# Gate table stored in stages of 64 tokens, kept activations stored from GpSimd's queue through three buffers

## The reference, cut to what matters

```python
def one(xb):
    qry = (xb @ wq).reshape(blk, PEER_HEADS, 2, PEER_DHALF)
    sc = jnp.einsum('thpd,hpkd->thpk', qry, subkeys).astype(F32)
    s1, i1 = lax.top_k(sc[:, :, 0], PEER_TOPK)
    s2, i2 = lax.top_k(sc[:, :, 1], PEER_TOPK)
    ...
    eid = e1 * PEER_NKEYS + e2
    g = jax.nn.softmax(sf, axis=-1)
    ug = jnp.take(u_tab, eid, axis=0)
    vg = jnp.take(v_tab, eid, axis=0)
    act = jax.nn.gelu(jnp.einsum('td,thkd->thk', xb, ug).astype(F32))
    return jnp.einsum('thk,thkd->td', (g * act).astype(xb.dtype), vg)
```

## Time and profile before

| what | value |
|---|---|
| median of 3 runs | 4225.2 us (4215.39 to 4245.17) |
| the profiled execution | 4207.73 us |
| its span, first to last instruction | 4206.1 us |
| mean granted TensorE clock | 0.962 of full speed |
| TensorE busy | 3867.2 us (92%) |
| VectorE busy | 2655.8 us (63%) |
| ScalarE busy | 1184.2 us (28%) |
| GpSimd busy | 671.5 us (16%) |
| the table of gates, gate_all | 28 stores of 2048 KB, 128 loads of 448 KB |
| the table of activations, act_all | 80 stores and 80 loads of 448 KB |

### The profile page before, as it was taken

How to read it: one execution, slowest core, us unless ns; L and a number is a source line. 1 busy time by engine, 2 the same in 40 slices (tenths; PEclk the granted TensorE clock), 3 DMA queues, 4 the chain that set the end, 5 groups by cost and what they waited for, 6 DMA issues and landing times. The chain is left out here.

```text
span 4206.1 us, 57139 instructions
## 1 busy us (share of the span) xinstructions
PE 3867.2 (92%) x21916; PEld 2051.7 (49%) x21916; DVE 2655.8 (63%) x4847; ACT 1184.2 (28%) x1707; POOL 671.5 (16%) x536
## 2 busy tenths in 40 slices
PE   5999787599969799989999997999999999999997
PEld 3676343166634544445555553444444444444443
DVE  5133111477655501989899975878777777777776
ACT  4233111144343301334334332222222222222223
POOL 0000000133201000000000002211111144444431
PEclk9999898799889899999999999999999999999999
DMA  5232541723163213889998879999999899999994
GB/s 206 95 118 79 148 120 46 267 78 100 55 217 130 88 52 103 218 236 293 290 269 239 228 215 280 276 253 246 240 246 245 230 271 289 274 288 284 274 254 122
DMA packets 975371, 837.17 MB, mean 199 GB/s; under 512 B 753730, under 2 KB 825754, under 8 KB 967707
## 3 DMA queue, kind: packets, MB, share of 16 engines
q1 hardware_dynamic: 912180, 564.40, 52.2%
q0 software_dynamic: 58960, 211.32, 14.8%
q10 hardware_dynamic: 4032, 58.72, 3.5%
HBM read 616.00 MB, written 181.85 MB: 190 GB/s over the span
## 5 line engine op out<-in xcount | busy, mean ns | idle before, releaser
L2920 PE MATMUL ex_psy<-ex_vhi,ex_wboth 128*128 128x512 f16 x3584 | 1077.3, 380 | 19.1 <-DVE ex_wboth L2779 13.5
L2888 PE MATMUL ex_psa<-h_hi,ex_uth 128*128 128x512 f16 (+1 forms) x2048 | 726.1, 355 | 33.7 <-DMA ex_utl<-ex_ulo 26.3
L2888 PE MATMUL ex_psa<-h_lo,ex_uth 128*128 128x512 f16 (+1 forms) x2048 | 725.7, 354 | 0.0
L2888 PE MATMUL ex_psa<-h_hi,ex_utl 128*128 128x512 f16 (+1 forms) x2048 | 725.2, 354 | 0.0
L2920 PE MATMUL ex_psy<-ex_vlo,ex_wboth 128*128 128x512 f16 x1792 | 681.1, 380 | 0.0
L2920 PEld LDWEIGHTS ex_psy<-ex_vhi,ex_wboth 128*128 128x128 f16 x3584 | 351.4, 98 | 444.3 <-DVE ex_wboth L2779 13.9
L2431 POOL DMA_INDIRECT ex_ug<-in_peer_u_dram,ex_idxp x128 | 152.4, 1190 | 1485.2 <-DVE ex_ug L2744 1063.4
L2740 DVE TENSOR_TENSOR ex_acc<-ex_acc,ex_psy 128x512 f32<-128x512 f32 x434 | 292.0, 682 | 145.3 <-PE ex_psy L2920 145.3
L2469 ACT ACTIVATE ex_wa<-ex_psa 128x512 f32<-128x512 f32 (+1 forms) x256 | 134.7, 542 | 671.9 <-PE ex_psa L2888 512.4
L2888 PEld LDWEIGHTS ex_psa<-h_hi,ex_uth 128*128 128x128 f16 x2048 | 201.0, 98 | 218.0 <-DMA ex_utl<-ex_ulo 29.4
L2888 PEld LDWEIGHTS ex_psa<-h_hi,ex_utl 128*128 128x128 f16 x2048 | 201.1, 98 | 190.0 <-issue 5.0
(11 more groups left out here) (387 smaller groups left out, 6108.1 us busy)
## 6 DMA issues: line engine op xcount, KB each, us to landing
ex_u<-in_peer_u_dram SPq DMA_DIRECT2D x128, 512.0 KB, 6.1
ex_v<-in_peer_v_dram SPq DMA_DIRECT2D x128, 512.0 KB, 5.6
gate_all<-rt_stage ACTq DMA_DIRECT2D x28, 2048.0 KB, 8.1
ex_gate<-gate_all SPq DMA_DIRECT2D x128, 448.0 KB, 7.7
act_all<-ex_wa SPq DMA_DIRECT2D x80, 448.0 KB, 3.3
ex_wa<-act_all SPq DMA_DIRECT2D x80, 448.0 KB, 5.5
ad_w<-in_ada_w_dram SPq DMA_DIRECT2D x8, 2048.0 KB, 10.3
sh_w<-in_w_in_dram SPq DMA_DIRECT2D x10, 1024.0 KB, 8.2
```

The source lines that it names most:

```text
L2888: mm = nc.tensor.matmul(ps_a[:, at:at + e - a], x[s][:, k, :], h[:, k, a:e], start=(k == 0 and j == 0), stop=(k == KD - 1 and j == 2))
L2920: mm = nc.tensor.matmul(sum_bank(q, n), w, v_[:, a * 512:(a + 1) * 512], start=(j == 0), stop=(j == len(mms) - 1))
```

## The change

1. `RUN` becomes 64: `gate_all` has 14 stages of 64 tokens, a stage buffer holds 8 groups, a store is 4096 KB (32 KB a partition), and there are 14 stores. A block's gates are read as 128 x 14 pieces of 256 bytes.
2. `keep` leaves SP. GpSimd's queue issues the 80 stores to `act_all`, in order, each behind its gelu. 
3. `wa` has a third buffer during the slots (`wa_third`); the gelu of block eb waits for the store of block eb - 3.
4. GpSimd comes to its first gathers only behind the 80 stores, and waits there also for the last evacuation (`evac`) and for both stage buffers to be stored. The six gathers of batch 0 move from slot 2 to group 0.
5. To make room, `cand` and `same` share their space (VectorE alone writes and reads both, in order), and `wa` and `st` move out of the region that the routing's buffers share.

```diff
--- before.py
+++ after.py
@@ -38,7 +38,7 @@
 NCH = P // CH
 HEADS, KEYS, TOPK, DHALF = 8, 128, 16, 128
 PICKS = HEADS * TOPK
-RUN = 32
+RUN = 64
 NEG = -1e30
 REC = DH + 2
 C_Q, C_K, C_V = 0, AW, 2 * AW
@@ -2209,8 +2209,9 @@
     YB = 4
     more = lambda eb, n: not isinstance(eb, int) or eb + n < KEYS
     two = lambda name: [pr.sem(f"ex_{name}{s}") for s in range(2)]
-    u_in, ut_in, g_in, wa_in, wa_stored = two("uin"), two("utin"), two("gin"), two("wain"), two("wastored")
+    u_in, ut_in, g_in, wa_in = two("uin"), two("utin"), two("gin"), two("wain")
     v_in = two("vin")
+    wa_stored = [pr.sem(f"ex_wastored{s}") for s in range(3)]
     (u_hi_done, u_lo_done, acted, gelu_done, w_done, w_hi_done, w_lo_done, v_hi_done, v_lo_done,
      y_done, added, ready) = (pr.sem(f"ex_{n}") for n in (
          "uhi", "ulo", "acted", "gelu", "w", "whi", "wlo", "vhi", "vlo", "y", "added", "ready"))
@@ -2241,18 +2242,22 @@
         gate_s, gate_up = sb("gates", [P, PAIRS]), sb("gateup", [NS, PAIRS])
         gate_g = sb("gateg", [P, PAIRS, 3])
         dots, gelus, weights = (sb(n, [P, 2 * EB, 3]) for n in ("dots", "gelus", "weights"))
+        wa = [sb(f"wa{s}", [P, DENSE]) for s in range(2)]
+        st = sb("st", [P, 6, PT + 1])
         with ExitStack() as early:
             ea = lambda name, shape, dt=F32: early.enter_context(nc.sbuf_tensor(f"rt_{name}", shape, dt))
             stage = [ea(f"stage{s}", [P, KEYS, RUN]) for s in range(2)]
+            wa_third = ea("wathird", [P, DENSE])
             sc, sc2 = ea("sc", [P, HP, KEYS]), ea("sc2", [P, HP, KEYS])
             top, ix = ea("top", [P, HP, TOPK]), ea("ix", [P, HP, TOPK], U32)
             ixf = ea("ixf", [P, HP, TOPK])
-            cand = ea("cand", [P, HEADS, TOPK * TOPK])
+            with nc.sbuf_tensor("rt_cand", [P, HEADS, TOPK * TOPK], F32) as cand:
+                pass
+            same = ea("same", [P, 2, HEADS, TOPK, TOPK], F16)
             best, ci = ea("best", [P, HEADS, TOPK]), ea("ci", [P, HEADS, TOPK], U32)
             c1, c2 = ea("c1", [P, HEADS, TOPK], U32), ea("c2", [P, HEADS, TOPK], U32)
             place = ea("place", [P, 2, HEADS, TOPK], F16)
             numbers = ea("numbers", [P, 2, HEADS, TOPK, TOPK], F16)
-            same = ea("same", [P, 2, HEADS, TOPK, TOPK], F16)
             ranks = ea("ranks", [P, TOPK, TOPK], F16)
             e12 = ea("e12", [P, 2, PICKS])
             ex, gate_t = ea("ex", [P, HEADS, TOPK]), ea("gatet", [P, HEADS, TOPK])
@@ -2268,9 +2273,8 @@
             v_hi, v_lo = ([sb(f"{n}{s}", [P, D], F16) for s in range(2 * EB)] for n in ("vhi", "vlo"))
             w_both = [sb(f"wboth{s}", [P, 2 * DENSE], F16) for s in range(2 * EB)]
             u, u_hi, u_lo, ut_h, ut_l = turns
-            wa = [sb(f"wa{s}", [P, DENSE]) for s in range(2)]
-            st = sb("st", [P, 6, PT + 1])
             ug, vg = ([sb(f"{n}{r}", [P, D]) for r in range(3)] for n in ("ug", "vg"))
+            wa_kept = wa + [wa_third]
             x_at = [u[0], u[1], ug[0], ug[1]]
             fg = ug[2]
             norm_rows = lambda p: P if NORM_M[p] < PT else NS
@@ -2338,10 +2342,6 @@
                         sp.wait_ge(sc_free, n)
                     r, a = rows_in(n), ROUTE[n] * P
                     sp.dma_start(sc[0:r, :, :].rearrange("p a k -> p (a k)"), t["scores"][a:a + r, :]).then_inc(sc_in, 16)
-
-                def keep(eb):
-                    sp.wait_ge(gelu_done, eb * 2 + 6)
-                    sp.dma_start(act_all[eb], wa[eb % 2][:, :]).then_inc(wa_stored[eb % 2], 16)
 
                 copies = window_copies(pr)
                 load_scores(0)
@@ -2357,13 +2357,9 @@
                         sp.wait_ge(picked, 7)
                         sp.dma_start(idx_s[NS:P, :], idx_up[:, :]).then_inc(moved, 16)
                         sp.dma_start(gate_s[NS:P, :], gate_up[:, :]).then_inc(moved, 16)
-                    if eb >= 2:
-                        keep(eb - 2)
                     for out, src in copies[eb:eb + 1]:
                         sp.dma_start(out, src).then_inc(copied, 16)
                 sp.wait_ge(copied, 16 * len(copies))
-                keep(AHEAD - 2)
-                keep(AHEAD - 1)
                 sp.wait_ge(routed, PT + 1)
 
                 def half(g1, g2, p, kept=False):
@@ -2373,8 +2369,8 @@
                         n, eb, s = g1 * EB + b, block_at(g1, b, kept), b % 2
                         if kept:
                             if isinstance(g1, int) and n == EB:
-                                sp.wait_ge(wa_stored[0], AHEAD // 2 * 16)
-                                sp.wait_ge(wa_stored[1], AHEAD // 2 * 16)
+                                for e in range(3):
+                                    sp.wait_ge(wa_stored[e], (AHEAD + 2 - e) // 3 * 16)
                             sp.wait_ge(w_lo_done, n + 1)
                             sp.dma_start(wa[s][:, :], act_all[eb]).then_inc(wa_in[s], 16)
                         else:
@@ -2440,8 +2436,14 @@
                             if dot + 1 < PAIRS:
                                 gather("peer_u", ug, u_rows, dot + 1, dotted)
 
+                for n, j, eb in slot_steps():
+                    pool.wait_ge(gelu_done, eb * 2 + 6)
+                    pool.dma_start(act_all[eb], wa_kept[eb % 3][:, :]).then_inc(wa_stored[eb % 3], 16)
                 pool.wait_ge(picked, 7)
                 pool.wait_ge(moved, 32)
+                pool.wait_ge(evac, GROUPS_A)
+                for e in range(2):
+                    pool.wait_ge(stage_stored[e], DENSE // RUN // 2 * 16)
                 gather("peer_u", ug, u_rows, 0, dotted)
                 run_unrolled(half)
 
@@ -2463,22 +2465,22 @@
                     nc.scalar.activation(u_hi[s][:, :, :], u[s][:, :].rearrange("p (k d) -> p k d", k=KD), ACT.Copy, scale=SPLIT)\
                         .then_inc(u_hi_done, 1)
 
-                def gelu(eb, s):
+                def gelu(eb, s, out):
                     for c, (a, e) in enumerate(SPANS):
                         act.wait_ge(acted, eb * 2 + c + 5)
-                        nc.scalar.activation(wa[s][:, a:e], ps_a[:, bank_of(c, s):bank_of(c, s) + e - a],
+                        nc.scalar.activation(out[:, a:e], ps_a[:, bank_of(c, s):bank_of(c, s) + e - a],
                                              ACT.Gelu_apprx_tanh, scale=1.0 / SPLIT).then_inc(gelu_done, 1)
 
                 def collect(g):
                     if not 0 <= g < GROUPS_A:
                         return
-                    m, q = g // 4, g % 4
+                    m, q = g // (RUN // BT), g % (RUN // BT)
                     act.wait_ge(scattered, g + 1)
                     if q == 0 and m >= 2:
                         act.wait_ge(stage_stored[m % 2], m // 2 * 16)
                     nc.scalar.activation(stage[m % 2][:, :, q * BT:(q + 1) * BT], ps_g[:, :, :].rearrange("p t e -> p e t"),
                                          ACT.Copy, scale=1.0 / GSCALE).then_inc(evac, 1)
-                    if q == 3:
+                    if q == RUN // BT - 1:
                         act.wait_ge(evac, g + 1)
                         act.dma_start(t["gate_all"][m], stage[m % 2][:, :, :])\
                             .then_inc(stage_stored[m % 2], 16)
@@ -2504,9 +2506,9 @@
                         expand(n)
                     if j == 7 * BLOCKS[n] // 8 and n <= PT:
                         exponent(n)
-                    if eb >= 2:
-                        act.wait_ge(wa_stored[eb % 2], eb // 2 * 16)
-                    gelu(eb, eb % 2)
+                    if eb >= 3:
+                        act.wait_ge(wa_stored[eb % 3], eb // 3 * 16)
+                    gelu(eb, eb % 2, wa_kept[eb % 3])
                     for g in groups_at(2 * eb):
                         collect(g)
 
@@ -2521,9 +2523,9 @@
                         nc.scalar.activation(v_hi[k][:, :], v[s][:, :], ACT.Copy, scale=SPLIT).then_inc(v_hi_done, 1)
                         if not kept:
                             if isinstance(g1, int) and n < 2:
-                                act.wait_ge(wa_stored[s], AHEAD // 2 * 16)
+                                act.wait_ge(wa_stored[s], (AHEAD + 2 - s) // 3 * 16)
                             act.wait_ge(w_lo_done, n + 1)
-                            gelu(eb, s)
+                            gelu(eb, s, wa[s])
                         act.wait_ge(w_done, n + 3)
                         nc.scalar.activation(w_both[k][:, 0:DENSE], wa[s][:, :], ACT.Copy).then_inc(w_hi_done, 1)
                         _, sums = gather_batches(g1, b, kept)
```

## The result

The changed kernel takes 4262.75 us (median of 5 runs, 4259.46 to 4266.75) against 4225.2 us for the kernel before (median of the 5 runs interleaved with them); the ratio is 1.0083, 95% interval 1.0056 to 1.0109. The profiled execution takes 4260.13 us, 52.4 us more than the profiled one before (spans 4258.5 and 4206.1).

A forecast was written before the change was run, and what follows sets the result against it. It took TensorE as the bound, fully busy from 2650 to 4140 us, with 77 us of idling elsewhere. Terms -6 + 12 - 15 + 6 = -3 us on a median of 4225.2 gave 4222 us, range 4175 to 4270.

The forecast's parts named there:

- Part 2: Slots 3 to 9: gate stores of 4 MB delay the transposes by 2.0 us each; 12 us slower, bounds 0 and 46.
- upper bound: Slots 3 to 9: 2.0 + 1.3 us a gate store, 46 us, if activations' stores also go ahead of the transposes.
- Part 1: Slots 3 to 9: third buffer and activations' stores off SP's queue save 6 us, bounds 0 and 10; GpSimd's queue costs nothing.
- floor of one clean tile: Tile from 2253 to 2354 us: TensorE idles 3.8 us because VectorE is late, though it waits only 0.2 us for ScalarE.
- third rival: GpSimd's stores are held up, landing after 22 us or more, so the third buffer doesn't help; 4300 us, chance 0.04.
- Part 3: Slots 0 to 2: moving the six gathers away removes the stall near 1800 us; 15 us saved, bounds 0 and 16.8.
- Part 4: Change-over into the groups: longer last store +3.6, gathers +10.6, fewer gate-load pieces and earlier loads -8; 6 us slower.
- Part 5: Gate loads of 256-byte pieces elsewhere change nothing, since TensorE is busy for 1490 of 1490 us.
- second rival: Behind each of 14 gate stores, the long store starves the transposes, 3.3 us each; sum +47, 4272 us, chance 0.17.
- signs of being wrong: Transpose waits absent or all 14 above 3 us, stall near 1800 us staying, or change-over moving by more than 15 us.

The follow-up runs named there:

- e1: The changed kernel with stages of 32 tokens again instead of 64, all else kept; ratio to the kernel before 1.0007 (0.997 to 1.0044).
- e3: The changed kernel with the stores of activations back on SP's queue behind the transposes; ratio to the kernel before 1.0079 (1.0051 to 1.0108).
- e7: The changed kernel with stages of 32 tokens and activations stored from SP's queue, third buffer and moved gathers kept; ratio to the kernel before 0.9992.
- e2: The kernel before with only the six first gathers moved to the change-over into the groups; ratio to the kernel before 1.0005 (0.9971 to 1.0039).
- e8: The kernel before with the six first gathers one at a time, each behind a gelu of its own; ratio to the kernel before 0.999 (0.9969 to 1.0011).

## Why the prediction was wrong

**Part 2 is the step that failed**, in its size: a term of +12 us where the long stages cost 47 (751 against 704 us in e1). Its mechanism and place were right. The store of 4 MB did take the engines for 10.0 us (forecast 10.6), each of the 13 stores inside B made TensorE wait, and the low transpose landed about 12 us behind its issue. Three things were mis-sized:

- The lateness of one transpose. I took 2.0 us; 42.5 us in 13 waits are 3.3 us each. That this is the figure of my upper bound is luck: its extra 1.3 us (1.2 by its own working) stood for the activations' store going ahead as well, and with those stores behind the transposes on SP's queue B is still 745 us (e3). Two readings behind the 2.0 were wrong and nearly cancel. I took the issue of the next pair, 2298.30, for the start of the next block; TensorE has scatter matmuls first and starts the block at 2300.24 (line below, kernel before), so the slack there was 5.2 us and not 3.3. And the landing moved by more than 5.3 us: from 10.5 us behind the store's issue before (2295.0 - 2284.49) to 17.3 (2354.7 - 2337.38), which is 6.8. With both right the sum for this place is 1.6 us, and 2.3 were measured. The rest is that I read one place for fourteen: in the block behind the store of 2148.8 the low transpose lands at 2160.2 and TensorE starts at 2161.73, a slack of 1.6 us, and in the changed kernel the longest of the 13 waits is 6.8 us.

```profile
2300.24 0.38 PE L2888 MATMUL ex_psa<-h_hi,ex_uth 128*128 128x512 f16 x1
```

- What covers it. I let more than half fall on VectorE's lateness. The one-hot waits are 24.0 us against 27.7 in e1, which differs by the stage alone: 3.7 us were covered. The argument with VectorE's load alone was wrong, since a late transpose also holds the `peer_u` load behind it and with it ScalarE's half of the next split (ScalarE waits 85.2 us for `peer_u`, 40.7 in e1).
- The clock. I priced it in parts 3 and 4 and forgot it here. The idle gaps of B brought the clock to 0.96, and the same matmuls took 15.7 us more than in e1, 20.4 more than before.

With 47 us in place of 12 the sum of -3 would have been +32, and 4257 us for the median.

**Part 1** had the wrong sign. ScalarE's waits went away as forecast and gave nothing, in e7 as well, where the third buffer came alone. The 7.3 us above the floor of one clean tile were not recovered: the one-hots have 29.0 us there. What I costed at nothing, the third queue, costs 6 to 9 us in three pairs. GpSimd's stores landed after 4.5 and 5.2 us (medians of the page) against 3.3 from SP's queue in e3, far from the 22 us of the third rival, which is out. That its stores now run beside the transposes and no longer behind them agrees with the later landings of the transposes (5.6 us in e1, 4.0 in e7), but no run separates this from other effects of the queue.

**Part 3** was right in mechanism, its size about half. The stall near 1800 us is gone, in the changed kernel and in e2. A became 9 us shorter, 7 in e2, not 15: transposes still end 4.5 us of TensorE's idling there, and TensorE now waits 2.8 us for VectorE's first gates.

**Part 4** was forecast at +6 and came at +4, but its terms are not confirmed. e2 shows +8 for the gathers alone at stages of 32. For stages of 64 in place of 32, one pair has 69 against 76 us (the changed kernel and e1), the other 74 against 71 (e3 and e7): what the longer last store costs and what the smaller number of pieces gives back can't be told from these.

**Part 5** holds: 1490 of 1490 us.

Stretch by stretch, the sum as measured is +9 for part 1 (B of e1 against before), +47 for part 2, -9 for part 3 and +4 for part 4, together the 51 us of the profiles. The range, 4175 to 4270, held the time. The second rival (4272) was the case that came, for the reason that it gave: the low transpose lands 14.4 us behind the issue of its pair (2354.7 - 2340.27), beyond the 10.9 at which it decides. That its sum of +47 came so near is partly luck: its 46 for part 2 rested on the wrong extra term and left out the clock, and its -3 and +14 for parts 1 and 4 are +9 and +4 in the runs. My choice between the ends of part 2 is what put the forecast on the wrong side: the slack and the length of the store came from one place in the trace, and I took a value near the favourable end. The signs of being wrong were badly drawn, too. The waits were neither absent nor all above 3 us (0.8 to 6.8), the stall went and the change-over moved by 4 us, so none of them appeared.

## What to carry to other kernels

A store that fills the DMA engines can hold back a short transfer issued beside it, however little that one moves; here a transpose landed 12.3 us behind its issue beside a store of 4 MB, and 5.5 us beside one of 2 MB. Before making a transfer longer, read how long behind its issue the most urgent neighbour lands and how much slack it has in all places, not one, and add the clock that each gap costs. If large stages are wanted for the reader's sake, store them in parts spread over the time in which the next stage fills; and a transfer moved away from a crowded place can cost its time again where it goes, as the gathers did (7 us won in A, 8 lost in C).

## What the runs showed of the hardware

- Packets of one 4 MB store were as long as the row of a partition, 32 KB; 8 or 4 KB packets gave a neighbour's 256-byte packets far more turns (222 for 18 per 1.08 MB, with 4 KB) and the store took longer, 15.5 against 13.1 us to landing. The waits for the neighbour fell by 4 us of 42, and TensorE's idling as a whole did not fall.
- A store of 448 KB issued from GpSimd's queue landed after 4.5 to 5.2 us (medians), from SP's after 3.3, and the low transposes on SP's queue landed later beside it, 5.6 against 4.0 us (e1 and e7).
- Halving the number of pieces of the gate loads lowered the DMA engines' share in the groups from 0.98 to 0.86 at the same GB/s, and the landing of such a load only from 7.7 to 6.7 us.
- The times of the kernels with whole stages of 64 spread less: 4259.46 to 4266.75 us in 5 runs of the changed kernel, 4254.64 to 4265.77 in 10 of e3, while the kernel before had 4202.04 to 4255.56 in 31. In the two profiles that were long for their kind (e1 and e8) the extra time was in the last groups, where TensorE waited for transposes and for VectorE's additions. Whether the pieces of the gate loads are the cause was not tried.
